# FFN up projections of a two-layer decoder: block products by sevens for every second pair of tiles

## The chip, the core and the metric

The kernel runs on one core of a Trainium2 chip. A core has five engines that run their own instruction streams and wait for each other by semaphores: TensorE (PE, matrix products into PSUM), VectorE (DVE), ScalarE (ACT), GpSimd (POOL) and SyncE (SP), which here issues all DMA transfers. The metric is the time of one execution in microseconds; it is the median of several runs.

## What is computed

The reference is a trunk of two layers over 16 meta and 1024 real tokens, each a row of 1024 numbers: a Mamba-2 mixer, then sliding-window attention, each followed by the same kind of feed-forward block (FFN). Only the up projection of the two FFN blocks is touched here, and the way the residual `h` is kept meanwhile.

```python
D_MODEL, D_FF, FFN_CONV, N_META = 1024, 2816, 3, 16

def conv_ffn(hn, w_up, conv_w, conv_b, w_down):
    u = causal_dwconv(hn @ w_up, conv_w, conv_b)      # (1040, 1024) @ (1024, 5632), then 3 taps along the tokens
    gate, val = u[..., :D_FF], u[..., D_FF:]
    return (jax.nn.silu(gate) * val) @ w_down

for i in range(DEPTH):
    ...                                               # mixer A or B, added to h
    ffn = conv_ffn(rms_norm(h, f_norm_pre[i]), f_w_up[i], f_conv_w[i], f_conv_b[i], f_w_down[i])
    h = h + rms_norm(ffn, f_norm_post[i])
```

## The kernel before

Tokens lie along the free dimension (1040 columns, in three blocks of 272, 384 and 384, `BLK`), features on the 128 partitions. All large products are done in three passes of float16: a number is split into a high half and a low half, and w_hi x_hi + w_hi x_lo + w_lo x_hi is summed in PSUM (`products`, L1828 to L1830). Weights are scaled by `WS` = 64 and split on the way: a unit of weights (128 outputs, 1024 inputs) comes by DMA into one of two `stage` buffers, ScalarE makes the high half (`split_hi`, L703), VectorE the low half (`split_lo`, L1285), and that gives the stage buffer back to SP (`w_lo`).

The up projection has 44 tiles of 128 outputs, taken as 22 pairs: tile 0 of a pair is a gate tile, tile 1 the value tile for the same hidden features. The first two pairs (the heads) are woven into the norm before; then `ffn_up` of TensorE runs pair 2 to 21 in a loop, for each tile three blocks of 8 x 3 products, tile 0 in PSUM banks 0 to 2, tile 1 in banks 3 to 5. Behind it a chain runs for each pair:
- ScalarE evacuates a tile into `UB` (`take`, L717), splits the next pair's unit (`split`, L703), does silu on the gate tile's taps (`gate`, L1137), and makes the high half of the hidden product (`hidden`, L1141).
- VectorE does the low half of the unit (L1285), then the three taps of the causal convolution over 1040 columns: one `tensor_scalar` with the bias (L1377) and two `scalar_tensor_tensor` (L1381). Behind tile 1's taps it multiplies gate and value (`product`, L1708).
- GpSimd makes the low half of the hidden product (`hidden_lo`, L650).

Each engine does this in the order in which it is written; nothing schedules it. The down projection follows (`two_unit` of TensorE): eight tiles whose contraction has 22 blocks, two units each; the hidden rows are read from `BIG`. Its first tile waits for `evac` three times ahead of its first product. The residual stays in SBUF in `hT` through all of this, and is updated behind the down projection (`post`, L1301 and L1306 of VectorE). `UB` holds the two tiles that the taps read, `T0`, `T1` and `T2` the taps' and the product's results.

The lines that matter for the order on TensorE and VectorE are these:

```python
with eng.Fori(0, KF - 2) as i:                       # TensorE, pairs 2 to 21
    for s_ in range(2):
        tile(i * 2 + (U_UP[layer] + 4 + s_), i * 6 + 3 * (J_UP[layer] + 4 + s_), s_, s_, x_r1)

def pair(i, width):                                  # VectorE
    for s_ in range(2):
        eng.wait_ge(evac, i * 6 + (6 + 3 * (j0 + s_) + 3))
        split_lo(i * 2 + (u0 + s_ + 3), s_, width)
        conv_tile(i, s_, UB[:, s_, :])
    product(i)
```

## Time and profile before

| | us |
|---|---|
| median of 3 runs (lowest, highest) | 2668.87 (2664.17, 2668.87) |
| the profiled execution's own time | 2665.41 |
| its span, first to last instruction | 2663.6 |
| FFN up of layer 0, pairs 2 to 21 | 423.2, from 896.8 to 1320.0 |
| FFN up of layer 1, pairs 2 to 21 | 423.0, from 2001.0 to 2424.0 |
| TensorE busy | 2590.4 |
| VectorE busy | 1486.6 |
| ScalarE busy | 945.3 |
| GpSimd busy | 634.0 |

The span is the profiled execution's, and all rows below come from it; a time of a row is counted from the start of the span. A row of a timeline gives start, duration, engine, line, operation, output and inputs, shapes, a count where rows were merged, and in square brackets how long the engine had stood idle and what ended that. Durations of following matrix products overlap, so their pace is read from the distance of their starts. PEclk is the granted clock of TensorE as a share of 2.4 GHz.

### The profile page before, as it was taken

The numbers are of one execution on the slowest core, as the hardware profiler recorded it, in microseconds if no ns is written. First come the engines' busy times: TensorE is split into PE (matmuls) and PEld (weight loads), VectorE is DVE, ScalarE is ACT, GpSimd is POOL, SyncE is SP. The second block draws the span as 40 slices with busy tenths as digits, with TensorE's granted clock in tenths as the row PEclk, the third lists the DMA queues.
The fourth block names the chain that finished last, engine by engine and source line by source line (L and its number), as shares of the span: only waits on it lengthen the run. The fifth ranks groups of instructions, "written<-read, shape, count | busy, mean of one in ns | idle before, by whom it ended". The sixth has DMA issues, their size and how long they took to land.

```text
span 2663.6 us, 43965 instructions
## 1 busy us (share of the span) xinstructions
PE 2590.4 (97%) x17944; PEld 1712.2 (64%) x17944; DVE 1486.6 (56%) x1882; ACT 945.3 (35%) x1739; POOL 634.0 (24%) x410
## 2 busy tenths in 40 slices
PE   8799999999999999999999998899999999999998
PEld 5466666666655666666666666676666666666665
DVE  6587777778687754455410266595376445443023
ACT  5333333343324423322311255596353332332121
POOL 1032544444242100000121211154411110001120
PEclk9899999999999999999999999998999999999999
DMA  3011111111131111111111112100111111111111
GB/s 119 32 33 41 34 39 41 32 33 36 37 128 32 32 55 47 47 54 49 59 48 50 49 33 56 40 2 9 40 41 55 47 47 55 47 50 55 54 54 64
DMA packets 38360, 125.00 MB, mean 47 GB/s; under 512 B 3424, under 2 KB 12768, under 8 KB 38240
## 3 DMA queue, kind: packets, MB, share of 16 engines
q1 hardware_dynamic: 38240, 123.31, 14.4%
q8 instruction: 86, 1.41, 0.2%
q14 instruction: 34, 0.28, 0.0%
HBM read 118.04 MB, written 4.19 MB: 46 GB/s over the span
## 4 chain that ended last, share of the span: by engine, by line
PE 83%; DVE 5%; ACT 4%; issue 3%; POOLq 2%; DMA 1%; DVEq 1%; POOL 1%; ACTq 0%
PE PS L1828 25%; PE PS L1829 24%; PE PS L1830 24%; PE PS L2076 1%; PE PS L2083 1%; ACT BIG L1225 1%; PE PS L2067 1%; PE PS L2106 1%; ACT BIG L1238 1%; DVE UB L1319 1%; POOLq L630 1%; PE PS L1915 1%; DMA stage<-wa 1%; PE PS L2094 1%; POOLq L628 1%
## 5 line engine op out<-in xcount | busy, mean ns | idle before, releaser
L1828 PE MATMUL PS<-R,whi 128*128 128x384 f16 (+1 forms) x3168 | 987.4, 312 | 1.1 <-DVE R L1796 1.0
L1829 PE MATMUL PS<-R,whi 128*128 128x384 f16 (+1 forms) x3168 | 987.0, 312 | 0.0
L1830 PE MATMUL PS<-R,wlo 128*128 128x384 f16 (+1 forms) x3168 | 986.6, 311 | 0.0
L1285 DVE SCALAR_TENSOR_TENSOR wlo<-stage,whi 128x1024 f16<-128x1024 f32 (+1 forms) x182 | 244.7, 1347 | 727.3 <-ACT whi L703 727.2
L1828 PE MATMUL PS<-BIG,whi 128*128 128x384 f16 (+1 forms) x1452 | 451.9, 311 | 7.9 <-issue 4.5
L1829 PE MATMUL PS<-BIG,whi 128*128 128x384 f16 (+1 forms) x1452 | 451.8, 311 | 0.0
L1830 PE MATMUL PS<-BIG,wlo 128*128 128x384 f16 (+1 forms) x1452 | 451.8, 311 | 0.0
L1828 PEld LDWEIGHTS PS<-R,whi 128*128 128x128 f16 x3168 | 311.2, 98 | 167.1 <-issue 13.7
L1829 PEld LDWEIGHTS PS<-R,whi 128*128 128x128 f16 x3168 | 311.2, 98 | 163.9 <-issue 10.8
L1830 PEld LDWEIGHTS PS<-R,wlo 128*128 128x128 f16 x3168 | 311.2, 98 | 157.3 <-issue 1.7
L650 POOL TENSOR_TENSOR BIG<-TT,BIG 128x1040 f32 x44 | 96.6, 2196 | 798.0 <-ACT BIG L1141 798.0
L703 ACT ACTIVATE whi<-stage 128x1024 f16<-128x1024 f32 (+1 forms) x182 | 199.3, 1097 | 143.0 <-PE PS L1830 138.8
L1381 DVE SCALAR_TENSOR_TENSOR TT<-UB,pr,TT 128x1040 f32<-128x1040 f32 x168 | 218.6, 1301 | 29.3 <-issue 28.1
L533 POOL TENSOR_TENSOR TT<-AUX,upper 128x1024 f16<-128x1024 f16 (+1 forms) x72 | 141.9, 1990 | 242.8 <-PE PS L2106 214.7
L1828 PEld LDWEIGHTS PS<-BIG,whi 128*128 128x128 f16 x1452 | 142.3, 98 | 84.2 <-issue 9.7
L1829 PEld LDWEIGHTS PS<-BIG,whi 128*128 128x128 f16 x1452 | 142.4, 98 | 72.7 <-issue 3.6
L1830 PEld LDWEIGHTS PS<-BIG,wlo 128*128 128x128 f16 x1452 | 142.4, 98 | 72.0 <-issue 1.0
L1141 ACT ACTIVATE BIG<-TT 128x1040 f32 (+1 forms) x44 | 47.1, 1070 | 285.8 <-DVE TT L1708 285.8
L806 ACT ACTIVATE UB<-PS 128x384 f32<-128x384 f32 (+1 forms) x120 | 54.7, 457 | 262.1 <-PE PS L1830 261.9
L607 POOL TENSOR_TENSOR TT<-R 128x384 f32<-128x384 f32 (+1 forms) x63 | 51.3, 831 | 397.4 <-ACT R L717 260.3
L717 ACT ACTIVATE UB<-PS 128x384 f32<-128x384 f32 (+1 forms) x240 | 99.8, 450 | 106.7 <-PE PS L1830 106.6
L1391 DVE SCALAR_TENSOR_TENSOR TT<-UB,pr,TT 128x1040 f32<-128x1040 f32 x72 | 101.3, 1407 | 47.9 <-ACT TT L814 43.9
(243 smaller groups left out, 3120.4 us busy)
## 6 DMA issues: line engine op xcount, KB each, us to landing
stage<-wa SPq DMA_DIRECT2D x164, 512.0 KB, 3.5
stage<-wd SPq DMA_DIRECT2D x32, 704.0 KB, 4.0
hT<-h SPq DMA_DIRECT2D x4, 1536.0 KB, 11.2
out<-hT SPq DMA_DIRECT2D x4, 768.0 KB, 3.5
hT<-h SPq DMA_DIRECT2D x2, 1088.0 KB, 9.9
BIG<-BIG SPq DMA_DIRECT2D x4, 260.0 KB, 7.1
out<-hT SPq DMA_DIRECT2D x2, 512.0 KB, 2.8
pr<-prm SPq DMA_DIRECT2D x1, 328.0 KB, 6.5
```

What stands on the lines that cost most here:

```text
L533: r = eng.tensor_tensor(aU[part][0:T, 0:HG * T].rearrange("p (h l) -> p h l", h=HG), ar_p[part][0:T, ds(g * HG + c * NH, HG)].unsqueeze(2) ...
L607: eng.tensor_tensor(T1[:, s:s + n], mix(m, b), mix(m, b), ALU.mult)
L650: eng.tensor_tensor(BIGh[:, ds(t, 1), L:2 * L], T2, BIGh[:, ds(t, 1), 0:L], ALU.subtract).then_inc(hid_lo, 1)
L703: eng.activation(WH[slot + 2 * aux][:, 0:width], stage[:, slot, 0:width], ACT.Copy, scale=WS).then_inc(w_hi, 1)
L717: r = eng.activation(dst, PS[:, 3 * st_ + b, 0:n], ACT.Copy, scale=scale)
L806: eng.activation(dst, PS[:, gemm_bank(i, b), 0:n], ACT.Copy, scale=scale).then_inc(evac, 1)
L1285: eng.scalar_tensor_tensor(out=WL[d][:, 0:width], in0=stage[:, slot, 0:width], scalar=WS, in1=WH[d][:, 0:width], op0=ALU.mult, op1=ALU.sub ...
L1381: r = eng.scalar_tensor_tensor(out=dst, in0=cin[:, o:o + L], scalar=prc(col + k), in1=dst, op0=ALU.mult, op1=ALU.add)
L1391: r = eng.scalar_tensor_tensor(out=T0, in0=UB[:, i % 2, o:o + L], scalar=prc(C_AW + (g * GT + j) * CONV_A + k), in1=T0, op0=ALU.mult, op1= ...
L1828: eng.matmul(acc, WH[slot][:, ws], x(0, k, b), start=first, stop=False)
L1829: eng.matmul(acc, WH[slot][:, ws], x(1, k, b), start=False, stop=False)
L1830: return eng.matmul(acc, WL[slot][:, ws], x(0, k, b), start=False, stop=last)
```

## The change

From pair 7 on every second pair (7, 9, ..., 21: eight in a layer) is done with Strassen's scheme in Winograd's form. The pair is one product of a 2 x 2 block matrix of weights (two tiles of 128 outputs by two halves of 512 inputs) with a 2 x 2 block matrix of tokens (two halves of 512 inputs by two halves of 520 tokens). Seven block products take the place of eight. Each has 4 x 3 products of TensorE for 272 and as many for 248 columns (`PIECE`). Pairs 2 to 6 stay as they were, and plain pairs 8, 10, ..., 20 stand between the seven pairs. This needs:
- Token sums: four sums of token blocks for each of four 128-row groups. GpSimd computes them into `BIG` (`token_sums`), ScalarE and VectorE split them into halves (`token_hi`, `token_lo`) that lie in `hT`. So `hT` is written to a DRAM tensor `h_keep` ahead of that, by one transfer of 4.26 MB, and read back by three transfers after the last seven pair, between the down projection's first two units and the rest.
- Weight operands: three blocks as loaded and four sums, seven in all of 512 columns. GpSimd makes the sums out of the stage buffers (`weight_sums`), ScalarE and VectorE the halves (`op_high`, `op_low`), into `AUX`. This is done during the plain pair ahead of a seven pair. GpSimd overwrites one buffer `tmp` and two of the stage blocks, so the last two sums wait for four low halves.
- The seven results stand in PSUM banks 0 to 6 in turn. ScalarE evacuates the first, VectorE adds the others from PSUM into `UB` (14 operations). ScalarE does the first tap with the bias for both tiles (`up_tap`), VectorE the other two.

The core of the diff:

```diff
@@ SP
-            load(wa, KD * P, U_UP[0], U_UP[0], KF)
-            load(wd, KU * P, U_DN[0], 0, KD)
+            def load_up(layer, row):
+
+                load(wa, KD * P, U_UP[layer], row, 3)
+                eng.wait_ge(h_new, 24 * (2 * layer + 1))
+                eng.dma_start(h_keep, hT[:, :, :]).then_inc(h_kept, 16)
+                load(wa, KD * P, U_UP[layer] + 6, row + 6, KF - 3)
+
+            def load_down(layer):
+
+                load(wd, KU * P, U_DN[layer], 2 * KD * layer, 1)
+                eng.wait_ge(seven, 14 * NS * (layer + 1))
+                eng.wait_ge(h_kept, 16 * (layer + 1))
+                for b in ORD:
+                    s, n = BLK[b]
+                    eng.dma_start(hT[:, :, s:s + n], h_keep[:, :, s:s + n]).then_inc(h_in[b], 16)
+                load(wd, KU * P, U_DN[layer] + 2, 2 * KD * layer + 2, KD - 1)
...
@@ GpSimd
+                for t in range(SF - 2):
+                    if t < KH:
+                        token_sums(t)
+                    hidden_lo(layer, t)
+                weight_sums(layer, 0, 0, lambda: hidden_lo(layer, SF - 2))
+                hidden_lo(layer, SF - 1)
+                with eng.Fori(0, NS - 1) as m:
+                    weight_sums(layer, m, 1, lambda: hidden_lo(layer, m * 2 + SF))
+                    hidden_lo(layer, m * 2 + (SF + 1))
+                hidden_lo(layer, KF - 1)
...
@@ ScalarE
+            def seven_pair(layer, m, i0, c0, gate, hidden, split_next):
...
+                eng.wait_ge(conv[1], i + c0)
+                for q in range(2):
+                    eng.wait_ge(seven, m * 14 + (14 * n + 1 + q))
+                    eng.activation(up_out(1, q, False), PS[:, q, 0:PIECE[q][1]], ACT.Copy,
+                                   scale=1.0 / WS).then_inc(seven_a, 1)
+                split_next(0)
+                split_next(1)
+                eng.drain()
+                eng.wait_ge(seven_v, m * 14 + (14 * n + 12))
+                up_tap(layer, m, i0, 0)
+                eng.drain()
+                eng.wait_ge(seven_v, m * 14 + (14 * n + 14))
+                up_tap(layer, m, i0, 1)
+                eng.drain()
+                eng.sem_inc(evac, 6)
+                gate(i)
+                hidden(i)
...
+                token_hi(layer, 0)
+                token_hi(layer, 1)
...
+                    for o in (A11, A12, A22, S1):
+                        op_high(layer, m, i0, o)
+                    take(i, 0, i)
+                    for o in (S3, S2, S4):
+                        op_high(layer, m, i0, o)
+                    gate(i)
+                    take(i, 1, i)
+                    hidden(i)
+
+                last_plain(0, 0)
+                token_hi(layer, 2)
+                token_hi(layer, 3)
...
@@ VectorE
+                add(12, 0, c12[0], u4[0])
+                up_taps(layer, m, i0, 0, (1,))
+                add(12, 1, c12[1], u4[1])
+                up_taps(layer, m, i0, 0, (0,))
+                up_taps(layer, m, i0, 1, (1, 0))
+                product(i)
...
@@ TensorE
+            def seven_pair(layer, m, i0):
...
+                eng.wait_ge(w_lo, m * 4 + (U_UP[layer] + 2 * (SF + 2 * i0) + 2))
...
+                for q in range(2):
+                    eng.wait_ge(evac, m * 12 + (kept + q + 1))
+                    multiply(0, q, A11, lambda part, kk, q: x_left(part, kk, q))
+                if i0 == 0:
+                    eng.wait_ge(t_lo, 4 * (layer + 1))
+                for q in range(2):
+                    eng.wait_ge(evac, m * 12 + (kept + 3 + q))
+                    multiply(2, q, S2, turn(T_2))
...
+                with eng.Fori(0, NS - 1) as m:
+                    seven_pair(layer, m, 0)
+                    for s_ in range(2):
+                        after_seven(layer, m, s_)
+                seven_pair(layer, 0, NS - 1)
```

Where the work stands now is seen best in the order of instructions. First VectorE around the first seven pair. Before, behind the head's tiles, a turn of the loop of one pair (register work between left out by "..."):

```order
L1285 SCALAR_TENSOR_TENSOR wlo<-stage,whi 128x1024 [waits w_hi]
...
L1377 TENSOR_SCALAR TT<-UB,pr 128x1040
...
L1381 SCALAR_TENSOR_TENSOR TT<-UB,pr,TT 128x1040
...
L1708 TENSOR_TENSOR TT<-TT 128x1040 [waits hid_lo,gate_act]
L1726 REGISTER_ALU
L1726 COMPARE_AND_BRANCH
```

Now, from the end of pair 5 to the first adds of pair 7 (L1896 is `token_lo`, L1902 `op_low`, L1928 an add from PSUM):

```order
L1969 TENSOR_TENSOR TT<-TT 128x1040 [waits hid_lo,gate_act]
...
L1896 TENSOR_TENSOR hT<-BIG,hT 128x2080 [waits t_hi] x2
L1902 SCALAR_TENSOR_TENSOR AUX<-stage,AUX 128x512 [waits op_hi] x3
L1902 SCALAR_TENSOR_TENSOR AUX<-BIG,AUX 128x512 [waits op_hi]
L1573 TENSOR_SCALAR TT<-UB,pr 128x1040 [waits evac]
L1577 SCALAR_TENSOR_TENSOR TT<-UB,pr,TT 128x1040 x2
L1902 SCALAR_TENSOR_TENSOR AUX<-stage,AUX 128x512 [waits op_hi]
L1902 SCALAR_TENSOR_TENSOR AUX<-BIG,AUX 128x512 [waits op_hi]
...
L1969 TENSOR_TENSOR TT<-TT 128x1040 [waits hid_lo,gate_act]
L1896 TENSOR_TENSOR hT<-BIG,hT 128x2080 [waits t_hi] x2
...
L1928 SCALAR_TENSOR_TENSOR UB<-PS,UB 128x272 [waits seven_a]
```

The halves of the operands stand on both sides of tile 0's taps, and the last two token parts behind the product of pair 6.

Second, TensorE at the start of the down projection. Before, behind pair 21's last block:

```order
L1830 MATMUL PS<-R,wlo 128x384
L2211 REGISTER_ALU
L2211 COMPARE_AND_BRANCH
L1889 UNCONDITIONAL_BRANCH
L1889 ISA
L1875 REGISTER_ALU [waits evac] x2
L1877 ISA [waits evac]
L1828 MATMUL PS<-BIG,whi 128x272 [waits hid_lo,w_lo]
```

Now, behind the last block of the last seven pair:

```order
L2509 MATMUL PS<-R,AUX 128x248 [waits seven_v]
L2510 MATMUL PS<-R,AUX 128x248
L2511 MATMUL PS<-R,AUX 128x248
...
L2168 UNCONDITIONAL_BRANCH
L2168 ISA
L2154 REGISTER_ALU [waits evac] x2
L2156 ISA [waits evac]
L2107 MATMUL PS<-BIG,whi 128x272 [waits hid_lo,w_lo]
```

The down tile's waits are the same; what stands ahead of them is a seven pair, whose six counts of `evac` ScalarE gives at once, behind its second `up_tap`.

## Rows read from the trace of the kernel before

**Rows 1.** The page, first part: busy time, share of the span, instructions.

```profile
PE 2590.4 (97%) x17944; PEld 1712.2 (64%) x17944; DVE 1486.6 (56%) x1882; ACT 945.3 (35%) x1739; POOL 634.0 (24%) x410
```

**Rows 2.** Stretches: length, busy time of each engine (instructions), PEclk, DMA share, GB/s.

```profile
896.80:1320.00 423.20, 423.20 (x2881) 281.80 (x2882) 222.65 (x187) 129.94 (x203) 46.16 (x21) 1.00 0.17 52
...
2001.00:2424.00 423.00, 423.00 (x2879) 281.51 (x2878) 220.39 (x186) 127.69 (x199) 45.66 (x21) 1.00 0.16 52
```

**Rows 3.** Timeline of TensorE: short products, and the starts of two tiles.

```profile
41.98 2.18 PE L2035 MATMUL PS<-BIG,R 128*128 128x32 f16 x81
...
1002.59 0.28 PE L1828 MATMUL PS<-R,whi 128*128 128x272 f16 x1
...
1013.17 0.28 PE L1828 MATMUL PS<-R,whi 128*128 128x272 f16 x1
```

**Rows 4.** Timeline of VectorE over one pair of layer 0.

```profile
946.23 1.24 DVE L1708 TENSOR_TENSOR TT<-TT 128x1040 f32<-128x1040 f32 x1 [0.23 <-issue]
951.36 1.22 DVE L1285 SCALAR_TENSOR_TENSOR wlo<-stage,whi 128x1024 f16<-128x1024 f32 x1 [3.89 <-ACT whi L703]
952.89 0.82 DVE L1377 TENSOR_SCALAR TT<-UB,pr 128x1040 f32<-128x1040 f32 x1 [0.31 <-issue]
953.88 1.30 DVE L1381 SCALAR_TENSOR_TENSOR TT<-UB,pr,TT 128x1040 f32<-128x1040 f32 x1 [0.17 <-issue]
...
967.39 1.24 DVE L1708 TENSOR_TENSOR TT<-TT 128x1040 f32<-128x1040 f32 x1 [0.23 <-issue]
```

**Rows 5.** Timeline of ScalarE in the same pair.

```profile
960.47 0.49 ACT L717 ACTIVATE UB<-PS 128x384 f32<-128x384 f32 x1 [1.92 <-PE PS L1830]
960.86 1.05 ACT L703 ACTIVATE whi<-stage 128x1024 f16<-128x1024 f32 x1
...
968.76 1.07 ACT L1141 ACTIVATE BIG<-TT 128x1040 f32 x1 [6.85 <-DVE TT L1708]
```

**Rows 6.** Groups by line; the last is one line's own view (min/median/max ns).

```profile
L703 ACT ACTIVATE whi<-stage 128x1408 f16<-128x1408 f32 x28 | 38.4, 1372 | 123.3 <-PE PS L1830 123.3
L814 ACT ACTIVATE TT<-UB,pr 128x1040 f32<-128x1040 f32 x24 | 30.1, 1253 | 10.3 <-DVE BIG L1405 8.4
...
L607 POOL TENSOR_TENSOR TT<-R x63: 638/826/1741, 761.3 to 2644.7; 128x384 f32<-128x384 f32 x42, 128x272 f32<-128x272 f32 x21
```

**Rows 7.** Timeline of VectorE where GpSimd works beside it.

```profile
678.02 0.69 DVE L1502 TENSOR_TENSOR AUX<-PS,AUX 128x512 f32<-128x512 f32 x1 [0.71 <-PE PS L2067]
...
903.85 4.42 DVE L1381 SCALAR_TENSOR_TENSOR TT<-BIG,pr,TT 128x1040 f32<-128x1040 f32 x2
...
913.25 1.22 DVE L1285 SCALAR_TENSOR_TENSOR wlo<-stage,whi 128x1024 f16<-128x1024 f32 x1
914.82 2.56 DVE L1377 TENSOR_SCALAR TT<-UB,pr 128x1040 f32<-128x1040 f32 x1 [0.34 <-issue]
```

**Rows 8.** Timeline of GpSimd at the same times.

```profile
678.07 1.04 POOL L541 TENSOR_TENSOR AUX<-AUX 128x512 f32<-128x512 f32 x1 [6.74 <-PE PS L2067]
...
904.18 2.99 POOL L650 TENSOR_TENSOR BIG<-TT,BIG 128x1040 f32 x1 [19.25 <-ACT BIG L1141]
...
914.65 2.16 POOL L650 TENSOR_TENSOR BIG<-TT,BIG 128x1040 f32 x1 [7.49 <-ACT BIG L1141]
```

**Rows 9.** Timeline of TensorE behind two idle times.

```profile
87.98 1.33 PE L2059 MATMUL PS<-BIG,onesD 128*128 128x288 f32 x2 [11.98 <-ACT AUX L1006]
...
522.62 1.71 PE L2067 MATMUL PS<-AUX,BIG 128*128 128x512 f32 x2 [2.31 <-ACT hT L864]
```

**Rows 10.** Stretches around these (columns as in rows 2; the clock is the third number from the end).

```profile
90.00:92.00 2.00, 2.00 (x10) 1.37 (x9) 1.65 (x2) 0.00 (x0) 0.00 (x0) 0.50 0.18 74
92.00:94.00 2.00, 2.00 (x15) 1.46 (x13) 0.00 (x0) 0.00 (x0) 0.00 (x0) 0.76 0.03 8
...
526.00:528.00 2.00, 2.00 (x13) 1.15 (x10) 2.00 (x3) 0.00 (x0) 0.00 (x0) 0.89 0.09 20
```

**Rows 11.** Timeline of SP: the residual's three loads before the first boundary.

```profile
760.42 4.30 SPq L444 DMA_DIRECT2D hT<-h  x3
```

**Rows 12.** A stretch while these transfers ran (columns as in rows 2).

```profile
770.00:775.00 5.00, 5.00 (x34) 3.07 (x33) 1.26 (x2) 0.00 (x0) 4.12 (x2) 1.00 1.09 391
```

250 lines of the change are left out of this document (231 added, 19 removed).

## The prediction, made before the changed kernel had run

> **What bounds the kernel now.** I read the page's first part, then the two FFN up stages by stretches, then the timelines of one pair of tiles, engine by engine. TensorE is busy for 97% of the span [rows 1], and in both up stages without a gap: 423.2 of 423.2 us and 423.0 of 423.0 us [rows 2]. So each microsecond of products that is taken out is gained, and each wait that is put in front of TensorE is lost one for one. A tile takes 10.58 us (1002.59 to 1013.17), 1040 columns times 24 products, so a pair takes 21.16 us and TensorE takes 2.36 columns a ns [rows 3]; VectorE's product shows the same beat (946.23 to 967.39, [rows 4]). In a beat VectorE works 2 x (1.22 + 0.82 + 2 x 1.30) + 1.24 = 10.5 us, ScalarE 6 us and GpSimd 2.2 us. They have room, but they are a chain: evacuate, taps, silu, product, high half, low half. The question is where the new waits stand in that chain.
>
> **Products removed.** A seven pair has 7 x 4 x 3 products of 272 and as many of 248 columns: 43,680 columns in place of 49,920. At the pace of [rows 3] that is 18.5 us for 21.2, 2.62 us less; eight pairs a layer save 20.9 us. Weight loads don't set the pace: 81 products of 32 columns, each with its load, started within 2.2 us [rows 3], and 248 columns need 105 ns. The cover of all else that the change adds is TensorE's own work, so I lay the rows end to end in the new order.
>
> **Start of the first seven pair.** Zero is the end of pair 6 on TensorE, where pair 7 would start if nothing held it. It needs all fourteen halves of its seven left operands (w_lo), and from its third product block on the four token parts (t_lo).
> - Pair 5's high half ends 11.6 us ahead of zero in the old beat: it ends at 969.83, and the next pair's products end 21.16 us after the last evacuation's bank was full at 960.3 [rows 5].
> - The token sums come ahead of that. One of the four sets is 4 adds of 384, 2 of 272 and 4 of 520 columns: 4 x 0.83 + 2 x 0.64 + 4 x 1.06 = 8.8 us on GpSimd [rows 6, 8]. GpSimd and VectorE exclude each other where both read two operands from SBUF: a bias row of 0.82 us took 2.56 until GpSimd's operation had ended, and two taps of 1.30 took 4.42 [rows 7, 8]. VectorE's adds from PSUM aren't held (0.69 us beside GpSimd's 1.04). A beat then holds 8.8 + 2.2 + 10.5 us of exclusive work and about 1.6 us of gaps, 23 us for 21.2, four times over; pair 4 and 5 win most of it back, and about 3.3 us are left. The copy ends at -8.3.
> - ScalarE then copies two token parts of 2080 columns. From 1.05 us for 1024 and 1.37 for 1408 columns [rows 5, 6] I get 1.95 each: -4.5. VectorE subtracts them at 2.3 each (twice 1.24, less one fixed part): -1.6.
> - Four low halves of 512 columns, 0.6 us apart (half of 1.22 plus a fixed part): +0.8. They stand in front of tile 6.0's taps, 3.8 us, into which GpSimd's two weight sums of 1.04 fall and cost 1.4: +6.0. Three low halves more: +7.9. TensorE starts here, 7.9 us late.
> - It does two blocks of products (2.65) and waits for t_lo. Behind +7.9 stand tile 6.1's taps and product (5.7), the high half (1.1), two token copies and the last subtraction, +21.4, as nothing of token parts 2 and 3 is done before pair 6 is through. That is a second wait of 10.9 us. In all 18.8 us a layer.
>
> **The loop of one seven and one plain pair.** TensorE has 18.5 + 21.2 = 39.7 us of work from zero, the start of the seven pair. The twelfth add ends at 17.1; first tap on ScalarE (1.25, [rows 6]), a tap on VectorE, the fourteenth add, ScalarE's second tap, two taps: 24.6; product 26.1; high half 27.3. GpSimd's low half of it holds VectorE to 29.6. Four low halves: 31.9. Plain tile 0's taps with GpSimd's two sums in them: 37.1. Three low halves: 38.8. So the next seven pair's operands are there 0.9 us before TensorE wants them, and the loop costs nothing. In a loop each wait on VectorE has register work ahead of it (gaps of 0.17 to 0.31 us, [rows 4]); I have counted them at the taps, but not at each low half and add. At 0.06 us each all the slack is used, at 0.1 it costs 0.5 us a pair. I take 0.7 us a layer for it, between 0 and 4.
>
> **Start of the down projection.** Its first tile waits for all six evacuations of pair 21 at once. In the seven pair ScalarE counts these only behind its second first-tap. TensorE's last block ends at 18.5, that tap at 21.3, with its drain 21.4: 2.9 us of wait a layer, where the old order had the bank free long before.
>
> **TensorE's clock.** After the 12 us wait at 76 to 88 us the products ran at the lower level (0.5, 1.2 GHz) from 88.0 until 93.0 [rows 9, 10]: 5 us at half pace, 2.5 us lost. After a wait of 2.3 us the clock was low up to 526.4, at most 1.7 us lost. Both new waits at the first seven pair count as the first case (one 2.5), the one of 2.9 us as the second (1.4): 3.9 us a layer, bounds 0 and 4.2. This is my largest choice after the token wait; I take the upper part, since both idle times of [rows 9] show it.
>
> **Moved transfers.** The residual (4.26 MB) is written after the heads and read back ahead of the down weights on SP's queue. The three loads of the same residual were issued in 4.3 us and moved at 391 GB/s [rows 11, 12], 11 us. The down units behind them land some 20 us after the up stage's end; TensorE wants them after one tile of 66 x 1040 columns there, 29 us, so 0. The same rate for the write lies under pairs 2 and 3: 0, at worst 3 us a layer.
>
> **Sum.** -20.9 + 18.8 + 0.7 + 2.9 + 3.9 = +5.4 us a layer, +10.8 in all, on 2665.4 us of the profiled execution: 2676. The three runs shown are 2664.2 and twice 2668.9; against their median it is 2680. I give 2677, nearer to the profiled execution's sum, since the third run lies there too.
>
> **A rule against the trace.** The rows show one of the two engines held to the other's end. The Trainium skill, "SBUF — State Buffer", section Who interferes with whom, says the same: VectorE with two SBUF inputs and a GpSimd instruction that reads SBUF use one port pair under an exclusive lock. By this rule, the trace agrees, the sum stands as it is; with the two side by side each layer would be 5 us shorter.
>
> **Rivals.**
> 1. The engines run side by side enough. Without the 3.3 us of backlog and the blocked operations the first wait is 2.9 in place of 7.9, and if the clock then is back at once, a layer gives -20.9 + 13.6 + 2.9 + 0 = -4.4: 2665.4 - 9 = 2657 to 2660, faster. Against it: [rows 7, 8] show the block in each overlap. With the clock lost it is 2664 to 2667, no change. It decides once the first two waits together are under 14 us.
> 2. The loop doesn't keep its slack. VectorE works 27 of the 39.7 us and is held for some 4 more. At 0.5 us a pair over 7 pairs a layer, with 0 to 4 us where the token sums hold up the weights of pair 3 (the low half of its first weights ends at 914.5 now [rows 7], and pair 3 starts at 896.8 + 21.2 = 918.0), it is 4 to 7 us a layer more: 2685 to 2694.
> 3. The clock stays up through the waits, the rest as forecast: 2669, no change.
> 4. The products don't get shorter, for columns in two pieces or instruction fetch (624 instructions a turn): then 42 us are missing, 2718. The down stage, with a larger loop body, runs 172.0 of 172.0 us busy [rows 2], so 2 in 100.
>
> **Chances.** Forecast 0.43, rival 2 0.25, rival 1 faster 0.12 and without change 0.08, rival 3 0.10, rival 4 0.02. Range 2661 to 2694. A measurement of this kernel tells about 0.2% (5.3 us) from no change. Faster by more 0.13, within 0.25, slower by more 0.62.
>
> **What would show it.** Right: in pair 7 an idle TensorE of some 8 us ahead of its first block and some 11 us ahead of its third; 2.9 us ahead of the down stage; a clock under 1 behind these; a seven pair of 18.5 us and no idle time at pairs 9 to 21. Wrong: one wait there under 5 us, a beat of 39.7 us that grows, or idle time inside the down stage.

## The result

The changed kernel takes 2696.03 us (median of 4 runs, 2693.2 to 2700.5), the kernel before beside it 2667.17: ratio 1.0113, interval 1.01 to 1.0125. It is slower by 1.1%. The forecast had the sign and most of the mechanism, but its time, 2677, is 19 us short, and the range ended at 2694.

The profiled execution has a span of 2696.7 us against 2663.6. The page's first part and the two up stages by stretches (columns as in rows 2; pairs 2 to 21, from the first of their products to the first of the down projection):

```profile
PE 2569.1 (95%) x18328; PEld 1757.2 (65%) x18328; DVE 1684.6 (62%) x2162; ACT 999.4 (37%) x1795; POOL 852.4 (32%) x554
```

```profile
897.90:1334.00 436.10, 409.90 (x3072) 301.94 (x3073) 322.55 (x330) 158.04 (x233) 145.73 (x86) 0.98 0.15 50
```

```profile
2011.10:2447.80 436.70, 409.66 (x3073) 301.76 (x3073) 324.69 (x330) 157.91 (x233) 145.34 (x86) 0.98 0.15 50
```

The stages were 423.2 us with no gap [rows 2]; they are 436.1 and 436.7, with TensorE idle for 26 and 27 us of each. VectorE works 100 us more in each stage, and GpSimd too.

Two things said ahead of the prediction and in it are put right here. The window of layer 1 in the table and in the second row of rows 2 lay 8 us late: that stage runs from 1993.1 to 2416.3, with the same 423.2 us, all busy. And the 172.0 us for the down stage of the kernel before stood in no row of rows 2; this is the row meant:

```profile
1320.00:1492.00 172.00, 172.00 (x1172) 114.56 (x1171) 29.52 (x18) 26.93 (x31) 33.19 (x22) 1.00 0.18 58
```

TensorE's timeline of the changed kernel, the starts that had an idle time ahead (in brackets, with what ended it):

```profile
920.40 0.29 PE L2107 MATMUL PS<-R,whi 128*128 128x272 f16 x1 [1.19 <-DVE wlo L1479]
...
963.83 0.29 PE L2107 MATMUL PS<-R,whi 128*128 128x272 f16 x1 [0.94 <-DVE wlo L1479]
...
975.27 0.29 PE L2107 MATMUL PS<-R,whi 128*128 128x272 f16 x1 [0.68 <-DVE wlo L1479]
...
1017.64 0.41 PE L2509 MATMUL PS<-R,AUX 128*128 128x272 f16 x1 [10.46 <-DVEq L1905]
...
1030.73 0.40 PE L2509 MATMUL PS<-hT,AUX 128*128 128x272 f16 x1 [7.95 <-DVE hT L1896]
...
1111.29 0.29 PE L2509 MATMUL PS<-R,AUX 128*128 128x272 f16 x1 [0.69 <-DVEq L1905]
...
1334.01 0.28 PE L2107 MATMUL PS<-BIG,whi 128*128 128x272 f16 x1 [3.01 <-ACTq L1284]
```

The clock behind the two large waits and behind the wait ahead of the down projection of either layer (third number from the end):

```profile
1017.60:1022.40 4.80, 4.75 (x23) 3.30 (x23) 4.22 (x4) 0.21 (x1) 0.00 (x0) 0.50 0.62 218
...
1030.70:1035.90 5.20, 5.17 (x25) 3.60 (x26) 0.44 (x1) 0.00 (x0) 0.00 (x0) 0.50 0.02 3
...
1334.00:1336.00 2.00, 1.99 (x14) 1.38 (x15) 1.93 (x2) 0.77 (x1) 0.00 (x0) 1.00 1.03 382
2447.80:2451.00 3.20, 3.19 (x16) 1.88 (x17) 2.60 (x3) 0.77 (x1) 0.00 (x0) 0.71 1.06 390
```

With these and the distance of the starts a layer can be added up. A seven pair at full clock takes 18.63 us, a plain pair 21.16. A "spell" is a stretch of products at the low clock behind a wait.

| term, us a layer | forecast | layer 0 | layer 1 |
|---|---|---|---|
| eight seven pairs, shorter by | -20.9 | -20.2 | -20.2 |
| waits at pairs 3 and 5 | 0 | 2.8 | 2.8 |
| pair 7, first block and third block | 7.9 + 10.9 | 10.5 + 8.0 | 10.4 + 8.2 |
| low clock in pair 7, behind the first and the second wait | 2.5 | 2.4 + 2.7 | 2.2 + 2.4 |
| loop (plain pairs over 21.16) | 0.7 | 3.1 | 3.9 |
| wait ahead of the down projection | 2.9 | 3.0 | 3.0 |
| low clock behind it | 1.4 | 0 | 1.7 |
| small gaps, the rest | 0 | 0.7 | 0.6 |
| sum | 5.4 | 13.0 | 15.0 |

That is 28 of the 33.1 us between the two profiles. The other 5.1 stand where nothing was changed: 1.1 ahead of the first up stage, 4.0 between the start of the first down projection and the second up stage; more on them below.

One row of the table must be read with care. From the first block of pair 7 to its third TensorE needs 13.09 us (1017.64 to 1030.73): 5.1 us for two blocks at half pace, 8.0 of wait. In all profiles of kernels with this pair of waits (changed, e2, e4, e5, e13) that distance is 13.07 to 13.09 us, while the wait in it goes from 7.7 to 8.9. So it is VectorE's work up to the token parts that sets it; products at full pace would only have waited longer. The first spell costs nothing, and the second wait without it would be 10.4 us, close to the 10.9 forecast.

### The profile page after: what moved, and what is told of

Read it like the earlier page. It is cut to its first block, busy times and chain, and to the rows that moved or that the text cites. A ratio compares the mean times of both kernels' runs of the same rounds, so it can differ in the third digit from the quotient of the medians.

```text
span 2696.7 us, 45633 instructions
## 1 busy us (share of the span) xinstructions
PE 2569.1 (95%) x18328; PEld 1757.2 (65%) x18328; DVE 1684.6 (62%) x2162; ACT 999.4 (37%) x1795; POOL 852.4 (32%) x554
## 4 chain that ended last, share of the span: by engine, by line
PE 67%; DVE 15%; ACT 6%; issue 5%; DVEq 4%; POOLq 2%; ACTq 1%; DMA 1%; POOL 1%
PE PS L2107 16%; PE PS L2108 16%; PE PS L2109 15%; DVE TT L1577 4%; PE PS L2509 3%; PE PS L2511 3%; PE PS L2510 3%; DVE TT L1573 1%; PE PS L2355 1%; PE PS L2362 1%; DVE TT L1917 1%; PE PS L2346 1%; PE PS L2385 1%; DVE wlo L1479 1%; ACT BIG L1419 1%
## 5 line engine op out<-in xcount | busy, mean ns | idle before, releaser
L2107 PE MATMUL PS<-R,whi 128*128 128x384 f16 (+1 forms) x2400 | 749.1, 312 | 6.7 <-DVE wlo L1479 5.7
L2108 PE MATMUL PS<-R,whi 128*128 128x384 f16 (+1 forms) x2400 | 748.6, 312 | 0.0
L2109 PE MATMUL PS<-R,wlo 128*128 128x384 f16 (+1 forms) x2400 | 748.1, 312 | 0.0
L2107 PEld LDWEIGHTS PS<-R,whi 128*128 128x128 f16 x2400 | 236.0, 98 | 136.2 <-issue 18.6
L2108 PEld LDWEIGHTS PS<-R,whi 128*128 128x128 f16 x2400 | 236.1, 98 | 124.8 <-issue 10.8
L2109 PEld LDWEIGHTS PS<-R,wlo 128*128 128x128 f16 x2400 | 236.0, 98 | 119.7 <-issue 1.7
L827 ACT ACTIVATE whi<-stage 128x1024 f16<-128x1024 f32 (+1 forms) x150 | 164.4, 1111 | 154.4 <-PE PS L2109 150.1
L723 POOL TENSOR_TENSOR BIG<-TT,BIG 128x1040 f32 (+1 forms) x44 | 99.1, 2252 | 382.8 <-ACT BIG L1314 381.5
L1577 DVE SCALAR_TENSOR_TENSOR TT<-UB,pr,TT 128x1040 f32<-128x1040 f32 x104 | 168.2, 1617 | 17.3 <-issue 16.0
L2509 PE MATMUL PS<-hT,AUX 128*128 128x272 f16 (+1 forms) x512 | 142.6, 279 | 16.1 <-DVE hT L1896 16.1
L930 ACT ACTIVATE UB<-PS 128x384 f32<-128x384 f32 (+1 forms) x120 | 54.7, 457 | 262.0 <-PE PS L2109 261.8
L1928 DVE SCALAR_TENSOR_TENSOR UB<-PS,UB 128x272 f32<-128x272 f32 (+1 forms) x224 | 92.1, 425 | 82.2 <-PE PS L2511 55.3
L2510 PE MATMUL PS<-hT,AUX 128*128 128x272 f16 (+1 forms) x512 | 142.6, 279 | 0.0
```

Of the source, the lines that this page charges most:

```text
L723: eng.tensor_tensor(BIGh[:, ds(t, 1), L:2 * L], T2, BIGh[:, ds(t, 1), 0:L], ALU.subtract).then_inc(hid_lo, 1)
L827: eng.activation(WH[slot + 2 * aux][:, 0:width], stage[:, slot, 0:width], ACT.Copy, scale=WS).then_inc(w_hi, 1)
L1577: r = eng.scalar_tensor_tensor(out=dst, in0=cin[:, o:o + L], scalar=prc(col + k), in1=dst, op0=ALU.mult, op1=ALU.add)
L1928: eng.scalar_tensor_tensor(out=dst, in0=PS[:, (e + q) % 7, 0:PIECE[q][1]], scalar=1.0 / WS, in1=term, op0=ALU.mult, op1=ALU.add).then_inc( ...
L2107: eng.matmul(acc, WH[slot][:, ws], x(0, k, b), start=first, stop=False)
L2108: eng.matmul(acc, WH[slot][:, ws], x(1, k, b), start=False, stop=False)
```

## Why VectorE is late at pair 7

VectorE's timeline over its work for pairs 2 to 5 (the number in brackets is its idle time and what ended it; L1969 is the product at the end of a pair), then at pair 7:

```profile
930.20 2.95 DVE L1577 SCALAR_TENSOR_TENSOR TT<-UB,pr,TT 128x1040 f32<-128x1040 f32 x1 [0.17 <-issue]
...
939.80 1.23 DVE L1479 SCALAR_TENSOR_TENSOR wlo<-stage,whi 128x1024 f16<-128x1024 f32 x1 [3.13 <-ACT whi L827]
...
950.36 1.44 DVE L1479 SCALAR_TENSOR_TENSOR wlo<-stage,whi 128x1024 f16<-128x1024 f32 x1 [3.13 <-ACT whi L827]
...
961.53 2.17 DVE L1479 SCALAR_TENSOR_TENSOR wlo<-stage,whi 128x1024 f16<-128x1024 f32 x1 [3.22 <-ACT whi L827]
...
979.36 1.24 DVE L1969 TENSOR_TENSOR TT<-TT 128x1040 f32<-128x1040 f32 x1 [0.23 <-issue]
...
997.87 2.02 DVE L1969 TENSOR_TENSOR TT<-TT 128x1040 f32<-128x1040 f32 x1 [0.23 <-issue]
1002.95 4.79 DVE L1896 TENSOR_TENSOR hT<-BIG,hT 128x2080 f16<-128x2080 f32 x2 [3.06 <-ACT hT L1244]
...
1010.26 1.79 DVE L1573 TENSOR_SCALAR TT<-UB,pr 128x1040 f32<-128x1040 f32 x1
1012.14 3.52 DVE L1577 SCALAR_TENSOR_TENSOR TT<-UB,pr,TT 128x1040 f32<-128x1040 f32 x2
```

GpSimd's timeline of two groups of token sums (the row counts six adds of 272 and 384 columns), and two of their adds of 520 columns, the first while VectorE stood idle, the second beside its low half:

```profile
932.01 7.83 POOL L731 TENSOR_TENSOR BIG<-R 128x272 f32<-128x272 f16 x6
...
950.68 9.27 POOL L731 TENSOR_TENSOR BIG<-R 128x272 f32<-128x272 f16 x6
960.09 1.29 POOL L736 TENSOR_TENSOR BIG<-BIG 128x520 f32<-128x520 f32 x1
...
962.76 2.10 POOL L739 TENSOR_TENSOR BIG<-BIG 128x520 f32<-128x520 f32 x1
```

And ScalarE's at the end of pair 4:

```profile
980.73 1.07 ACT L1314 ACTIVATE BIG<-TT 128x1040 f32 x1 [6.85 <-DVE TT L1969]
981.71 1.14 ACT L841 ACTIVATE UB<-PS 128x272 f32<-128x272 f32 x3
982.73 1.07 ACT L827 ACTIVATE whi<-stage 128x1024 f16<-128x1024 f32 x1
```

Three things can be read here. The two engines hold each other, as forecast: a tap takes up to 2.95 us for 1.30, and a group of sums takes 16 to 19 us for 9.7 (4.6, as forecast, and four adds at 1.28, for which I had taken 1.06). Second, VectorE stands idle for 3.13 us ahead of nearly each low half, in the middle of being late: ScalarE's hidden row (`hidden`, L1314) waits for VectorE's product, the evacuation (L841) and the split (L827) of the next unit stand behind that in ScalarE's order, and VectorE waits for the split: 1.07 + 1.14 + 1.07 less overlap, 3.1 us, and the same behind silu for the other tile. So a pair on VectorE takes 10.5 + 2 x 3.1 + gaps, some 18 us, while it is late. Pair 5, in which nothing of GpSimd's token sums is left, shows it: 18.5 us from product to product (979.36 to 997.87). VectorE wins back 2.7 us of 21.2, not the 9 that are left of 21.2 when only its 10.5 of work and 1.6 of gaps are counted. The forecast's "pair 4 and 5 win most of it back" left this chain out. Third, TensorE itself waited for late low halves at 920, 964 and 975. The experiments ask which of these carries the loss.

## The experiments

Theory A: the loss is in the order of steps ahead of the first seven pair, and a delay isn't won back because VectorE stands behind ScalarE's chain. Rival B: VectorE and GpSimd have too much exclusive work in pairs 2 to 6, wherever it stands. Rival C: the loss comes with each seven pair, or with the residual's transfers. The kernel before took 2664.5 to 2666.6 us in these sessions. "Stage" is the time from the last product of the norm ahead to the down projection's first product, 441.8 us in both layers of the kernel before, 454.7 and 455.2 in the changed one. A wait "at pair 5" stands ahead of the first product of one of its two tiles.

### Token parts earlier (e1_tokens_early)

```diff
                 hidden(2)
+                token_hi(layer, 0)
+                pair(3, KD * P)
+                token_hi(layer, 1)
+                pair(4, KD * P)
+                token_hi(layer, 2)
+                token_hi(layer, 3)
...
-                token_hi(layer, 0)
-                token_hi(layer, 1)
...
                 last_plain(0, 0)
-                token_hi(layer, 2)
-                token_hi(layer, 3)
```

(VectorE's `token_lo` likewise.)

> Only the place of the token parts is changed: ScalarE's copy and VectorE's subtraction of group 0 stand behind pair 2, of group 1 behind pair 3, of groups 2 and 3 behind pair 4, in place of two behind pair 5 and two behind pair 6. Theory A (the loss sits in VectorE's and ScalarE's own order ahead of pair 7): the second wait (8.0 us in the changed kernel) is gone, the first (10.5) is 5 to 7 us shorter since two copies and two subtractions no longer stand ahead of the operands, and one of the two spells of low clock (5.05 us lost together) goes. 14 to 18 us a layer less, some 2660 to 2670 us. Theory B (VectorE and GpSimd together have too much work in pairs 2 to 6, wherever it stands): the waits only move, TensorE idles 15 us or more a layer ahead of pair 7's third block, 2685 or more. Both: waits at pairs 3 and 5 (2.8 us) as they were or 1 to 3 us longer.

2679.6 us, ratio 1.006 (1.0047 to 1.0074); stage 447.3 and 448.0. TensorE, layer 0:

```profile
966.49 0.29 PE L2112 MATMUL PS<-R,whi 128*128 128x272 f16 x1 [4.20 <-DVE wlo L1481]
...
1017.26 0.40 PE L2514 MATMUL PS<-R,AUX 128*128 128x272 f16 x1 [5.72 <-DVEq L1907]
```

The second wait is gone and the first fell to 5.7, as A said, but pairs 4 to 6 now wait 2.64, 4.20 and 0.72 us (2.63, 2.77 and 2.40 in layer 1), with one spell among them in each layer. Half of the gain only changed place: 7.4 and 7.2 us a layer where A said 14 to 18. That is a miss, and a point for B, or for the chain.

### Without the token sums (e2_no_token_sums)

```diff
-                for i in range(2):
-                    for b, (a, n) in enumerate(BLK):
...
+                eng.memset(t_sums(kk), 0.0)
                 eng.drain().then_inc(t_sum, 1)
```

> GpSimd's ten adds of each group of token sums are left out and one memset stands in their place, so the products of the sums are of zeros; all else, the token parts' copies included, is as in the changed kernel. If VectorE is held by GpSimd's sums (the rows of pairs 2 to 5: taps of 1.30 us took 1.7 to 2.9), the waits at pairs 3 and 5 (2.8 us a layer) go, VectorE's taps are back at 1.30, and the first wait of pair 7 is 2 to 4 us shorter (the backlog): 5 to 7 us a layer less, with the second wait unchanged at 8: some 2682 to 2686 us. If the backlog has nothing to do with the sums: within 3 us of the changed kernel's 2696.

2680.9 us (2674.1 to 2682.2), ratio 1.005 (1.0034 to 1.0065); stage 445.6 and 447.2. No wait at pairs 3 to 5, and at pair 7:

```profile
1009.54 0.41 PE L2496 MATMUL PS<-R,AUX 128*128 128x272 f16 x1 [5.55 <-DVEq L1892]
...
1022.62 0.41 PE L2496 MATMUL PS<-hT,AUX 128*128 128x272 f16 x1 [8.92 <-DVE hT L1883]
```

So GpSimd's sums cost the 2.8 us at pairs 3 and 5 and 4.9 us of the first wait, 8 to 9 us a layer and so more than the 5 to 7 expected. But 14.5 us of wait stay with all of GpSimd's token sums gone: the larger part of pair 7's loss isn't the shared work. The 3.13 us ahead of VectorE's low halves stand in this trace too, with every tap at 1.30: pair 3 takes it 18.6 us. B as the main cause is weakened here; e10 below decides it.

### TensorE waits for each block's operand (e3_fine_waits)

```diff
-                eng.wait_ge(w_lo, m * 4 + (U_UP[layer] + 2 * (SF + 2 * i0) + 2))
-
                 def multiply(e, q, o, moving):
+                    if q == 0:
+                        eng.wait_ge(op_lo, m * 7 + (7 * n + o + 1))
```

> TensorE no longer waits ahead of a seven pair for all seven left operands, but ahead of each block for that block's own (the first block needs the first, the second token block the sixth, the last the seventh). Theory A (the loop's 3.05 us a layer and the first wait are waits for the last three low halves): the loop's waits of 0.4 to 0.9 us at every second seven pair go, all 3 us a layer of them; pair 7's first block starts when its bank and first low half are there, some 8 us earlier, but the wait for the token parts grows by as much, so that nothing is gained there beyond 0 to 2 us. 3 to 5 us a layer less: some 2686 to 2690 us. Rival (the beat of the double pair is set by VectorE's total work, 39.7 us and more): the wait moves behind, to the sixth operand or to the plain pair, and the loop keeps its 3 us: 2694 to 2696.

2687.35 us, ratio 1.0083 (1.007 to 1.0097); stage 451.7 and 451.3.

```profile
1009.04 0.29 PE L2509 MATMUL PS<-R,AUX 128*128 128x272 f16 x1 [1.24 <-DVE AUX L1902]
...
1031.49 0.41 PE L2509 MATMUL PS<-hT,AUX 128*128 128x272 f16 x1 [19.62 <-DVE hT L1896]
```

As expected: the first wait moved into the second (20.9 us together; the waits at pairs 3 and 5 are as they were), and the loop runs at 39.78 us (18.62 + 21.16) with no gap. The loop's loss was the demand for all seven operands at once. The long wait cost no more clock than each of the shorter two: one spell, 2.7 us. Still, pairs 6 and 7 together take 63.5 us here and 63.4 in the changed kernel, with one spell and with two: the first of the two cost nothing.

### The evacuations counted earlier (e4_evac_early)

```diff
+                eng.sem_inc(evac, 6)
                 up_tap(layer, m, i0, 1)
                 eng.drain()
-                eng.sem_inc(evac, 6)
```

> ScalarE counts the six evacuations of a seven pair ahead of its second first-tap, not behind it and its drain. Theory A: the wait ahead of the down projection (3.01 us in both layers) gets shorter by that tap, 1.3 us, to 1.7; behind layer 1's the clock fell (1.6 us lost), which may go. 2.6 to 4.3 us less in all, 2692 to 2693.5 us. Rival (something else is last there, hid_lo or the down weights): the wait stays at 3.0 and the time at 2696.

2689.9 us, ratio 1.0095 (1.008 to 1.0111). The wait ahead of the down projection is 1.73 us in both layers:

```profile
1327.87 0.28 PE L2107 MATMUL PS<-BIG,whi 128*128 128x272 f16 x1 [1.73 <-ACTq L1283]
```

The forecast's term is right, and no low clock follows this wait in either layer of any of the six kernels with it (the time from layer 1's to the end of the span is 247.2 to 247.5 us, 247.2 in the kernel before and 248.9 in the changed one). Behind the wait of 3.0 us the clock fell in 7 of 14 cases (seven profiles, two layers), at a price of 1.4 to 3.0 us. The tap and the clock were put at 2.6 to 4.3 us. The medians differ by 6.1, and 2689.9 lies under the 2692 expected; in its second profile (e14) the changed kernel lost 3.0 and 1.7 us of clock there, so the term itself can come to 7.3.

### Short weight sums (e5_short_weight_sums)

```diff
-                eng.tensor_tensor(tmp, a21, a22, ALU.add).then_inc(op_sum, 1)
+                eng.tensor_tensor(tmp[:, 0:4], a21[:, 0:4], a22[:, 0:4], ALU.add).then_inc(op_sum, 1)
```

(and the other three likewise)

> The changed kernel with GpSimd's four weight sums of a seven pair cut to 4 of their 512 columns (the sums' operands then hold other numbers); orders, waits and counts are as they were. Theory A (the loop's 3.05 us a layer come from VectorE's taps being held by two weight sums, and from the low halves waiting for them): the waits at pairs 11, 15 and 19 go, the loop costs under 0.7 us, and pair 7's first wait is 1 to 3 us shorter: 3.5 to 5.5 us a layer less, 2685 to 2689. Rival (VectorE's own work fills the 39.7 us): the loop's waits stay, only the first wait is shorter: 2691 to 2694.

2681.1 us, ratio 1.0054 (1.0039 to 1.007); stage 448.6 and 449.1, so 6.1 us a layer less, a little over what was expected. No gap in the loop, and the first wait of pair 7 is 7.93. In the loop, VectorE of the changed kernel, and of this one:

```profile
1089.42 1.98 DVE L1917 SCALAR_TENSOR_TENSOR TT<-UB,pr,TT 128x1040 f32<-128x1040 f32 x1 [0.78 <-ACT TT L1265]
...
1104.11 1.49 DVE L1573 TENSOR_SCALAR TT<-UB,pr 128x1040 f32<-128x1040 f32 x1 [0.42 <-issue]
1105.78 2.04 DVE L1577 SCALAR_TENSOR_TENSOR TT<-UB,pr,TT 128x1040 f32<-128x1040 f32 x1 [0.18 <-issue]
```

```profile
1099.13 0.82 DVE L1573 TENSOR_SCALAR TT<-UB,pr 128x1040 f32<-128x1040 f32 x1 [0.42 <-issue]
1100.13 1.30 DVE L1577 SCALAR_TENSOR_TENSOR TT<-UB,pr,TT 128x1040 f32<-128x1040 f32 x1 [0.18 <-issue]
```

Two weight sums beside the plain tile's taps cost VectorE 1.4 us, the forecast's own figure. What the forecast left out are the other two. The first pair of sums can fall on the first tap of the seven pair (L1917), and where it does, that tap takes 1.7 to 2.2 us for 1.30. In the changed kernel's profile this happens in pairs 9, 13 and 17 of layer 0 and 9, 11, 15 and 19 of layer 1, and all seven of TensorE's waits of over 0.4 us in the two loops stand ahead of the seven pair that comes next (11, 15, 19; 11, 13, 17, 21). At pair 11 the last low half ends 40.5 us behind pair 9's start, not 38.8: 0.7 of that is the held tap, the rest gaps that were not counted. So the slack of 0.9 us was gone. The Trainium skill, "SBUF — State Buffer", section Who interferes with whom, has VectorE with two SBUF inputs contend with a GpSimd instruction that reads SBUF; here the trace agrees (2.04 for 1.30). The bias row L1573 with its one tile of input is held as well (1.49 for 0.82).

### The three edits together, with eight and with two seven pairs (e6_all, e7_all_sf19)

e6_all is the sum of the edits of e1, e3 and e4. e7_all_sf19 has on top of it:

```diff
-SF = 7
+SF = 19
```

> The three edits of the first runs together: token parts behind pairs 2, 3 and 4, TensorE's waits for each block's own operand, the six evacuations counted ahead of the second first-tap. If the three add up: the run with the early parts had 5.7 us ahead of pair 7; that falls by a block of 2.65 and a low half to 2.4, with less clock lost behind it (2.3), the loop's 2.8 us go, the down wait is 1.7. The waits at pairs 3 to 5 (8.7 us) and the clock behind them (2.6) stay. 8 to 10 us a layer less than that run's 2679.6: 2658 to 2664, level with the kernel before (2664.6) or up to 0.2% faster. If one eats the other (the waits all hang on one overloaded VectorE): 2668 or more.

> The combined kernel with only two seven pairs a layer (19 and 21) in place of eight; token sums, token parts, the residual's way through memory and all waits stand where they did. A seven pair saves 2.53 us where nothing is late. If the loss is a fixed cost of the preparation, it stays whole: the combined kernel's time plus 6 x 2.53 x 2 = 30 us, less 1 to 4 us for a first seven pair whose operands no longer come behind a backlog: 26 to 30 us over the combined kernel. If the loss grows with the number of seven pairs (the loop), the difference is under 22 us.

e6_all: 2661.2 us, ratio 0.9983 (0.9974 to 0.9992), stage 437.9 in both layers: as expected, and the first version that beats the kernel before. Its waits in layer 0 are 1.17, 2.63, 3.03 and 0.72 ahead of pairs 3 to 6, and 2.38 and 0.48 inside pair 7.

e7_all_sf19: 2683.9 us, ratio 1.0067 (1.0053 to 1.0081), stage 449.9 in both. Six pairs fewer cost 12.0 us a layer in the stage, not 15.2: each of the six still brings 2.53 us, and the difference is pair 7's own loss (2.9 us of waits in e6_all), which pair 19 hasn't got. The other waits stay whole (7.5 and 9.0 us at pairs 3 to 6, with two seven pairs). So the loss of e6_all is fixed: at eight seven pairs it is 16 us a layer, at two some 13. The medians differ by 22.7 us and the stages by 24, less than the 26 to 30 expected for a fixed loss and barely over the 22 of the other theory; it is the waits in the traces that decide. C's first half falls for all but one term: the changed kernel's loop loss, 3.1 and 3.9 us a layer over seven plain pairs, does come with the pairs, and e6_all no longer has it, since it holds e3's edit.

### Sums spread, first seven pair at 9 (e8_sf9_spread)

```diff
-SF = 7
+SF = 9
+SUMS = (0, 2, 3, 5)
+PARTS = (2, 4, 5, 7)
...
-                    if t < KH:
-                        token_sums(t)
                     hidden_lo(layer, t)
+                    if t in SUMS:
+                        token_sums(SUMS.index(t))
...
-                        take(i, s_, i)
+                        eng.wait_ge(acc_ready, i * 6 + 3 * (j0 + s_) + 3)
                         split(i, s_, width)
+                        take(i, s_, i)
```

> The combined kernel with the first seven pair at 9 (seven a layer), GpSimd's four groups of token sums behind the hidden rows of pairs 0, 2, 3 and 5 in place of ahead of those of 0 to 3, the token parts behind pairs 2, 4, 5 and 7, and ScalarE's split of a unit ahead of its evacuations. Theory A (VectorE can't win a delay back, since it stands 3.1 us a tile behind ScalarE's hidden row, evacuations and split; the sums one after another pile it up): the waits at pairs 3 to 5 (8.7 us) and the clock behind them go down to 0 to 3 us, the first seven pair starts 0 to 2.5 us late; one seven pair less costs 2.5. A layer's stage is then 7 to 12 us shorter than the combined kernel's: 2640 to 2650 us, faster than the kernel before. Rival (exclusive work of both engines, the same in sum, is what counts): as long as the combined kernel or up to 5 us longer.

2655.6 us, ratio 0.9959 (0.9945 to 0.9973); stage 435.1 and 435.4. Faster, yet 6 us short of the expectation. One wait of 2.59 us stays ahead of pair 6, and one of 3.90 (2.44 in layer 1) in pair 9; a low clock follows both waits of pair 9, but that of pair 6 only in layer 1. VectorE still stands 3.13 us idle ahead of a low half (2.96 where a token part comes first), since silu, hidden row and token part remain ahead of ScalarE's split: spreading the work without mending the chain was half a cure.

### ScalarE's order (e10_act_order_sf7, e11_act_order_sf9, e13_act_order_only)

```diff
                 def pair(i, width):
                     for s_ in range(2):
-                        take(i, s_, i)
+                        eng.wait_ge(acc_ready, i * 6 + 3 * (j0 + s_) + 3)
                         split(i, s_, width)
+                        take(i, s_, i)
                         if s_ == 0:
-                            gate(i)
-                    hidden(i)
+                            hidden(i - 1)
+                        for kk in PARTS.get((i, s_), ()):
+                            token_hi(layer, kk)
+                    gate(i)
```

e10_act_order_sf7 and e11_act_order_sf9 have this with the edits of e3 and e4, and the token parts behind a tile of the pairs ahead (`PARTS`); e11 also has SF = 9 and the spread sums. e13_act_order_only has it alone, its token parts where the change put them.

> The combined kernel (first seven pair at 7, sums where they were) with ScalarE's order in pairs 3 to 6 changed: split of the unit, evacuation, then the hidden row of the pair before; silu behind the second evacuation; token parts behind the first or second tile of pairs 3, 4 and 5. Theory A (VectorE stands 3 us a tile behind ScalarE's hidden row, evacuation and split, so a delay isn't won back): these waits go, VectorE gets the delay back within a tile or two, and the waits at pairs 3 to 5 (8.7 us with the clock's 2.6) go down to 1 to 4; a layer's stage from 437.9 to 428 to 432: 2641 to 2650 us. Rival (exclusive work of VectorE and GpSimd is what fills pairs 2 to 6): the waits change place, stage 435 or more, 2655 or more.

> The same order of ScalarE with the first seven pair at 9 and the sums spread over pairs 0, 2, 3 and 5. Theory A: no wait ahead of pair 9 beyond 1 us, 1.5 to 3 us in its third block for the sixth operand, no low clock behind it or one spell (2.4); stage 428 to 432, 2641 to 2650. Rival: 435 as in the spread kernel without the new order (2655.6).

> The changed kernel with only ScalarE's order in pairs 3 to 5 changed (split, evacuation, then the hidden row of the pair before, silu behind the second evacuation); token parts, TensorE's waits and the down start stay as they were. Theory A (the delay of VectorE isn't won back because it stands behind ScalarE's chain): the waits at pair 5 (0.94 and 0.68 us) go, the first wait of pair 7 falls from 10.5 to 3 to 6 us, the second stays at 8: stage 446 to 449 in place of 454.7, 2678 to 2686 us. Rival (the early token parts did it): stage within 2 us of 454.7.

| kernel | us | ratio (interval) | stage, layers 0 and 1 |
|---|---|---|---|
| e13_act_order_only | 2679.6 | 1.0054 (1.0037 to 1.0071) | 448.1, 448.1 |
| e10_act_order_sf7 | 2640.8 | 0.9901 (0.9885 to 0.9918) | 427.4, 427.2 |
| e11_act_order_sf9 | 2635.8 | 0.9881 (0.9865 to 0.9898) | 425.9, 425.9 |

Alone, the order takes 6.6 and 7.1 us off a layer: the waits at pair 5 are gone and the first wait of pair 7 fell from 10.46 to 5.59, the second stayed (8.02), as expected. With e3's and e4's edits in both, e10 takes 10.5 us a layer off e6_all, with GpSimd's sums all still there; its token parts also stand later and one by one behind tiles, so the 10.5 isn't the order's alone. B had 435 us or more for this stage; with 427.4 it falls as the main cause. e10 and e11 came out a little faster than A had them (428 to 432 us of stage). In e10, VectorE goes from token part to low half to taps without standing idle, though it is still held (4.27 for a token part of 2.3):

```profile
962.15 3.02 DVE L1897 TENSOR_TENSOR hT<-BIG,hT 128x2080 f16<-128x2080 f32 x1
965.10 2.30 DVE L1480 SCALAR_TENSOR_TENSOR wlo<-stage,whi 128x1024 f16<-128x1024 f32 x1
967.50 1.61 DVE L1574 TENSOR_SCALAR TT<-UB,pr 128x1040 f32<-128x1040 f32 x1
969.18 4.45 DVE L1578 SCALAR_TENSOR_TENSOR TT<-UB,pr,TT 128x1040 f32<-128x1040 f32 x2
973.55 4.27 DVE L1897 TENSOR_TENSOR hT<-BIG,hT 128x2080 f16<-128x2080 f32 x1
```

In e11 the stage has one wait left, and TensorE is busy for all but that of it:

```profile
896.50:1303.80 407.30, 405.57 (x3049) 298.15 (x3050) 330.71 (x312) 154.00 (x229) 161.95 (x89) 1.00 0.16 53
```

```profile
1303.79 0.28 PE L2107 MATMUL PS<-BIG,whi 128*128 128x272 f16 x1 [1.73 <-ACTq L1285]
```

441.8 less seven times 2.53 plus 1.7 is 425.8; measured 425.9. The seven products bring just what the forecast's first term says when nothing else is late. Nothing is left out of this kernel, and it is 1.2% faster than the kernel before.

### The residual's way alone, and both kernels once more (e12_residual_only, e0_before_again, e14_changed_again)

e12_residual_only is the kernel before with `load_up` and `load_down` of the change's diff; the reload waits for `evac` of pair 21 in place of `seven`. The other two are unchanged kernels.

> The kernel before, no seven pairs, with the residual alone moved: written to memory behind the third pair of units, read back between the down projection's first two units and the rest. If the transfers are hidden, as the forecast has them (0, at worst 3 us a layer): within 1.5 us of the kernel before, TensorE without idle time in either up stage. If they cost (weights behind them late, or the stretch between the first down projection and the second up stage, 2.4 to 4.7 us longer in the changed kernels, hangs on them): 3 to 8 us more, with idle time on the down weights or a longer stretch there.

> The kernel before, profiled once more. The stretch from the first down projection to the second up stage took 654.6 us in its first profile and 656.1 to 659.3 in the changed kernels, by a low clock behind waits that were there before. If that is chance between executions, this profile shows 655 to 659 us there too; if it belongs to the changed kernels, 654.6 again.

> The changed kernel, profiled once more. If the longer stretch between the first down projection and the second up stage is chance between executions, it may lie anywhere from 654.6 to 660 us, in this profile as in the others; if it belongs to the changed kernel, 658 to 659 again. The up stages 454.7 and 455.2 within 0.5 us.

e12: 2666.14 us, ratio 0.9998 (0.9989 to 1.0008), TensorE without a gap in the stage:

```profile
896.70:1319.90 423.20, 423.20 (x2882) 281.77 (x2881) 222.73 (x187) 129.90 (x203) 46.17 (x21) 1.00 0.16 51
```

As expected. The transfers are hidden; C's second half falls, and the forecast's 0 was right.

e0 took 2669.08 us and e14 2695.39. The spans of their profiles differ by 26.1 us, where the first two differ by 33.1. e14's stages are 454.5 and 453.7 us; layer 1's is 1.5 shorter than before and so outside the half microsecond that was expected, for a shorter second spell and a cheaper loop (3.2 for 3.9). The first up stage starts at 896.8 and 898.9 us in the kernel before and at 897.9 and 894.4 in the changed one: the 1.1 us ahead of it are chance.

The stretch between the first down projection and the second up stage: 654.6, 656.3 and 656.3 us in the three profiles without seven pairs, 656.1 to 660.6 in the thirteen with them (658.6 and 660.6 in the changed kernel; 3.0 of e14's 660.6 are the low clock behind the down wait, which lies in this stretch). It takes on different values in the same kernel, so part of it is chance. Stretches of the kernel before, then of the changed kernel, at the same place of the program:

```profile
1612.00:1616.00 4.00, 3.18 (x11) 1.49 (x12) 3.99 (x7) 2.17 (x4) 0.00 (x0) 0.50 0.56 141
1616.00:1620.00 4.00, 4.00 (x19) 2.15 (x18) 4.00 (x8) 1.92 (x5) 2.25 (x2) 0.66 0.89 230
```

```profile
1625.00:1629.00 4.00, 2.16 (x7) 1.05 (x8) 3.62 (x6) 2.18 (x4) 0.00 (x0) 0.69 0.27 75
1630.00:1634.00 4.00, 4.00 (x27) 2.54 (x26) 4.00 (x8) 1.91 (x5) 2.23 (x2) 1.00 0.88 231
...
1644.00:1649.00 5.00, 4.94 (x22) 2.81 (x23) 2.96 (x6) 2.48 (x7) 0.40 (x3) 0.70 0.01 2
```

Both fall to a low clock around a wait of 4.5 us (it ends at 1612.8 and 1626.8); the changed kernel comes back sooner, reaches the next wait 1.4 us earlier (3.40 us for 2.04), and then runs at a lower clock behind it. A wait that both kernels have costs clock in one and not in the other. Why the kernels with seven pairs meet the dearer case more often is open: no run sets where the clock stands at that moment. It is worth 2 to 4 of the 29 us between the medians.

## The prediction against the runs

- **Products.** Right: 18.63 us a pair for the 18.5 forecast; 2.53 saved, not 2.62, which is 0.7 us a layer.
- **What failed first: "pair 4 and 5 win most of it back", with "about 3.3 us are left".** VectorE late by a few microseconds wins back 3 a pair, not 9, for the 3.1 us it stands behind ScalarE's chain in each tile. So TensorE waited 2.8 us at pairs 3 and 5, which the forecast had only as part of a rival (0 to 4 at pair 3), and pair 7's first wait was 10.5 us, not 7.9. That is 5.4 us a layer, the largest part of the miss. The sums' own share of the first wait is 4.9 us (e2), where 3.3 were taken; the other 1.0 us of its excess has no run of its own. e13 shows what the chain is worth, 6.6 us a layer; e2 what the sums are, 8 to 9. The two overlap and don't add up.
- **Start of the first seven pair.** The two waits and their causes stood where the forecast put them, and their sum (18.4 and 18.5 us) is near its 18.8. That is luck: the first came out 2.6 us longer, and the second is shorter by the 2.4 us that the low clock took out of it.
- **Clock.** Taken as one spell of 2.5 us in pair 7. It fell behind both waits, 4.6 to 5.1 us, over the bound of 4.2; but the first spell cost no time, and the second, which did, measured 2.7 and 2.4. Behind the down wait it was 0 and 1.7 for 1.4, and 3.0 and 1.7 in the second profile.
- **Loop: the second step that failed.** Forecast 0.7, bounds 0 and 4; measured 3.1 and 3.9. The order laid out was right (e5 removes the sums and the loss, e3 the wait and the loss). Its slack of 0.9 us left out that the first two weight sums can hold a tap as well (0.4 to 0.9 us where they do), and the gaps between instructions.
- **Down projection.** 2.9 forecast, 3.01 measured; e4 confirms the cause.
- **Moved transfers.** 0, confirmed by e12.
- **The rivals.** Rival 2 named the right additions, loop and pair 3, but it left pair 7 as forecast. Its own figures, 4 to 7 us a layer on 2677, give 2685 to 2691; 2694 needs the base of 2680. Rivals 1, 3 and 4 did not occur.
- **The range.** The large terms that were short pointed the same way (a late VectorE makes waits at pairs 3 and 5, a longer one at pair 7 and a dearer loop); I had set their bounds as if each were alone. The layers came out 7.6 and 9.6 us over the forecast; with the 5.1 us elsewhere that leads from its 2676.2 to 2698.5, and the profiled execution took 2698.66. Some of the 5.1 is chance, as the second profiles show.

## What to carry to other kernels

When an engine has slack by its busy time, look at how it stands while it is late: a wait on another engine's in-order queue at each step, 3.1 us here, takes the slack away just when it is needed. If work is added to such a chain, first put the step that others wait for (the split) ahead of the step that waits (the hidden row). That order alone brought the changed kernel from 1.1% slower to 0.5% slower; with the token parts made earlier, the operands waited for one by one and the evacuations counted earlier, it became 1.0 to 1.2% faster. Add up costs that share a cause at their upper ends together. And ask of a low clock whether anyone waits for its products: a spell that ends in a wait for another engine costs nothing.
